# First norm of a decoder step computed on token rows instead of on the transposed input, and expert results read back by two issuing engines

## What is computed

```python
def rms_norm(x, g):
    y = x * lax.rsqrt(jnp.mean(x * x, axis=-1, keepdims=True) + NORM_EPS)
    return y * g

def chunk_spatial_gating(h, w_in, g_v, w_s, b_s, w_out):   # h = rms_norm(x, norm1[0])
    z = jax.nn.gelu(h @ w_in)                # w_in: 1024 x 2048
    u, v = z[..., :CHUNK_WIDTH], z[..., CHUNK_WIDTH:]
    v = rms_norm(v, g_v)
    s = (causal w_s) @ v + b_s               # per chunk of 128 rows and group of 256 columns
    return (u * s) @ w_out, v
# hp = hp + mixer(rms_norm(hp));  hp = hp + experts(rms_norm(hp))
```

## Time and profile before

| | |
|---|---|
| median of 3 runs | 731.02 us (727.8 to 733.04) |
| the profiled execution's own time | 725.12 us |
| its span, first to last instruction | 723.4 us |
| mean granted TensorE clock | 0.952 |
| TensorE products / weight loads busy | 620.2 us (86%) / 422.3 us (58%) |
| VectorE, ScalarE, GpSimd busy | 288.0, 128.8, 126.8 us |

### The profile page before, as it was taken

The page is one execution under the profiler, slowest core; times in us unless marked ns, Lnnn a source line. Parts: engine busy times, 40 slices in busy tenths (PEclk is TensorE's granted clock), DMA queues, the critical chain, the costliest instruction groups (busy, mean ns, idle before and its releaser), DMA issues.

```text
span 723.4 us, 11181 instructions
## 1 busy us (share of the span) xinstructions
PE 620.2 (86%) x4089; PEld 422.3 (58%) x4089; DVE 288.0 (40%) x837; ACT 128.8 (18%) x284; POOL 126.8 (18%) x178
## 2 busy tenths in 40 slices
PE   4899999968999988689999996976987899997730
PEld 2677777746655555566667764564756655564310
DVE  2321232175334422436675775430136434432224
ACT  2102011130111112101121553311114011111100
POOL 0000000002232322004223221320000232331213
PEclk9999999999999999799999999998998999999975
DMA  8985004075899993898333763799736589999633
GB/s 330 291 332 207 27 0 182 6 274 191 339 410 410 410 411 142 305 387 316 117 117 100 257 229 122 252 378 400 310 136 225 192 340 410 412 411 403 232 94 111
DMA packets 60283, 184.81 MB, mean 255 GB/s; under 512 B 11676, under 2 KB 12238, under 8 KB 56006
## 3 DMA queue, kind: packets, MB, share of 16 engines
q1 hardware_dynamic: 49030, 155.52, 57.2%
q0 software_dynamic: 11200, 28.60, 10.9%
HBM read 178.96 MB, written 13.50 MB: 266 GB/s over the span
## 4 chain that ended last, share of the span: by engine, by line
PE 68%; DMA 14%; DVE 9%; SPq 3%; issue 3%; ACT 2%; DVEq 0%; POOLq 0%; ACTq 0%
PE PS L1198 27%; PE PS L1277 11%; DMA hT<-in_moe_w_up 6%; PE PS L1299 6%; PE PS L1446 3%; SPq L367 3%; PE PS L1189 3%; DMA half_b<-in_b_w_o 3%; PE PS L1266 2%; DMA zT<-y_rows 2%; PE PS L1463 2%; DMA y_rows<-zT,where 1%; PE PS L1184 1%; PE PS L1288 1%; PE PS L1256 1%
## 5 line engine op out<-in xcount | busy, mean ns | idle before, releaser
L1198 PE MATMUL PS<-hT,half_b 128*128 128x288 f32 x384 | 101.5, 421 | 8.9 <-DMA half_b<-in_b_w_o 5.6
L1198 PEld LDWEIGHTS PS<-hT,half_b 128*128 128x128 f32 x384 | 74.4, 197 | 32.1 <-issue 10.4
L1198 PE MATMUL PS<-hT,half_a 128*128 128x288 f32 x256 | 66.9, 419 | 3.1 <-DVE hT L799 3.1
L1198 PEld LDWEIGHTS PS<-hT,half_a 128*128 128x128 f32 x256 | 48.7, 194 | 20.9 <-issue 4.1
L539 POOL DMA_INDIRECT y_rows<-zT,where x33 | 33.5, 1015 | 154.0 <-ACT zT L674 148.8
L1277 PE MATMUL PS<-ew_in,zT 128*64 128x256 f32 x480 | 56.0, 387 | 4.8 <-DMA ew_in<-in_moe_w_up 2.9
L942 DVE COPY zT<-PS 128x128 f32<-128x128 f32 x33 | 9.6, 291 | 117.9 <-PE PS L1288 87.7
L1277 PEld LDWEIGHTS PS<-ew_in,zT 128*64 128x64 f32 x480 | 36.7, 140 | 26.3 <-issue 12.6
L534 POOL DMA_INDIRECT zT<-h_rows,where x35 | 36.0, 1030 | 53.6 <-DVE where L911 31.0
L901 DVE TENSOR_SCALAR zT<-lanes,slots 128x128 bf16<-128x128 bf16 (+1 forms) x222 | 39.1, 248 | 1.8 <-DVE slots L964 1.3
L545 POOL DMA_DIRECT2D h_rows<-tokbuf x2 | 1.7, 832 | 216.5 <-ACT tokbuf L657 216.5
(11 more groups left out here) (278 smaller groups left out, 941.9 us busy)
## 6 DMA issues: line engine op xcount, KB each, us to landing
ew_in<-in_moe_w_gate SPq DMA_DIRECT2D x15, 1024.0 KB
ew_in<-in_moe_w_up SPq DMA_DIRECT2D x15, 1024.0 KB
ew_down<-in_moe_w_down SPq DMA_DIRECT2D x15, 1024.0 KB
half_b<-in_moe_w_gate SPq DMA_DIRECT2D x6, 1024.0 KB
half_b<-in_moe_w_up SPq DMA_DIRECT2D x6, 1024.0 KB
half_b<-in_moe_w_down SPq DMA_DIRECT2D x6, 1024.0 KB
half_a<-in_moe_w_gate SPq DMA_DIRECT2D x6, 1024.0 KB
half_a<-in_moe_w_up SPq DMA_DIRECT2D x6, 1024.0 KB
```

Source lines behind the costliest of these rows:

```text
L1198: mm = pe.matmul(PS[:, bank, 0:T], w[:, k, col:col + P], src[:, k, :], start=(k == 0), stop=(k == KT - 1))
```

## The change

The first norm is computed where its sum runs along the row: ScalarE squares the arriving token rows with a running sum, takes three roots' columns, VectorE makes reciprocals per row, and the rows are scaled into `x_scaled` (a view of `zT`), tile 1 by ScalarE, tiles 0 and 2 by VectorE. TensorE transposes the scaled rows, and VectorE applies the gains on the way from PSUM to `hT`. The mean-square products of this norm are gone. The unscaled rows, which the residual needs as `xT`, are transposed in a second set of 8 groups, one behind each V tile of the projection, and ScalarE copies them out between the gelus. Identity is loaded by itself ahead of the gains; the rest of the constants and `ws_in` come behind `w_a`, and the `ws_in` transposes behind the first projection tile. In both layers ScalarE issues the three k = 1 read-backs, SP the three others. The last sums are all VectorE's, and each row tile of the output is written when it is ready.

```diff
@@ SP
-            load(cst[:, :], t["consts"], S["const_in"])
+            load(ident, t["consts"][:, cols["ident"]], S["ident_in"])
...
-            load(ws_in, t["a_w_s"].rearrange("l g t s -> t (l g) s"), S["gains_in"])
             load(w_a, w_in[:, :, D:2 * D], S["w_v_in"])
+            load(cst[:, P:], t["consts"][:, P:], S["const_in"])
+            load(ws_in, t["a_w_s"].rearrange("l g t s -> t (l g) s"), S["const_in"])
             load(w_b, w_in[:, :, 0:D], S["w_u_in"])
...
                 for c, (at, m) in enumerate(tok):
-                    for k, dst in enumerate((tokbuf, y_second)):
-                        load(dst[0:m, c, :], y_dram[l][at:at + m, k, :], s_yb[c])
+                    load(tokbuf[0:m, c, :], y_dram[l][at:at + m, 0, :], s_yb[c])
...
-            sp.wait_ge(S["y_sum"], 1)
-            sp.wait_ge(S["y_sum_pool"], 1)
-            sp.dma_start(o["yp"].rearrange("a (c p) d -> p (a c) d", p=P), tokbuf[:, 0:CH, :]).then_inc(S["y_out"], 16)
-            sp.wait_ge(S["y_sum"], 2)
+            for c in range(CH):
+                sp.wait_ge(S["y_sum"], c + 1)
+                sp.dma_start(o["yp"].rearrange("a (c p) d -> p (a c) d", p=P)[:, c, :], tokbuf[:, c, :]).then_inc(S["y_out"], 16)
+            sp.wait_ge(S["y_sum"], NT)
@@ GpSimd (end)
-            pool.tensor_tensor(tokbuf[:, 1, :], tokbuf[:, 1, :], y_second[:, 1, :], ALU.add).then_inc(S["ysum"], 1)
-            pool.wait_ge(S["ysum"], 1)
-            pool.tensor_tensor(tokbuf[:, 1, :], tokbuf[:, 1, :], x_rows[1], ALU.add).then_inc(S["y_sum_pool"], 1)
@@ ScalarE
+                act.wait_ge(el["sc0"], scattered(LAST - 1)[1])
+                hold(el["sc1"], 16 * more + scattered(LAST - 2)[1])
+                hold(el["in1"], more_gathered(more))
+                hold(el["xt_sb"], more + NE)
+                for c, (at, m) in enumerate(tok):
+                    act.dma_start(y_second[0:m, c, :], y_dram[l][at:at + m, 1, :]).then_inc(s_yb[c], 16)
...
-            squares(0)
-            root(0)
+            ready_for(ACT.Sqrt)
+            act.wait_ge(S["x_in"], 32)
...
+            for c, (_, n) in enumerate(tok):
+                act.activation(squared[c], tokbuf[0:n, c, :], ACT.Square, accum_out=x_sums[0:n, c:c + 1]).then_inc(S["squared"], (3, 3, 2)[c])
+            act.wait_ge(S["squared"], KT)
+            act.activation(x_std[:, 0:CH], x_sums[:, 0:CH], ACT.Sqrt, bias=eps[:, :], scale=1.0 / D)
+            act.activation(x_std[0:TSA, CH:NT], x_sums[0:TSA, CH:NT], ACT.Sqrt, bias=eps[0:TSA, :], scale=1.0 / D).then_inc(S["rooted"], 1)
+            act.wait_ge(S["dve_step"], 1)
+            act.activation(x_scaled[:, 1, :], tokbuf[:, 1, :], ACT.Identity, scale=x_rec[:, 1:2]).then_inc(S["x_row"], 1)
 
             for j in range(2 * KT):
...
+                if j < KT:
+                    act.wait_ge(S["xr_t"], j + 1)
+                    act.copy(xT[:, j, :], PS[:, 4 + j % 2, 0:T]).then_inc(S["xr_sb"], 1)
@@ VectorE
+            dve.wait_ge(S["rooted"], 1)
+            dve.reciprocal(x_rec[:, 0:CH], x_std[:, 0:CH])
+            chain.link(dve.reciprocal(x_rec[0:TSA, CH:NT], x_std[0:TSA, CH:NT]))
+            for c in (0, CH):
+                n = tok[c][1]
+                dve.tensor_scalar(x_scaled[0:n, c, :], tokbuf[0:n, c, :], x_rec[0:n, c:c + 1], None, ALU.mult).then_inc(S["x_row"], 1)
...
-                dve.tensor_copy(xT[:, k, :], PS[:, k % 4, 0:T]).then_inc(S["xt_sb"], 1)
+                dve.tensor_scalar(hT[:, k, :], PS[:, k % 4, 0:T], gains[:, k:k + 1], None, ALU.mult).then_inc(S["normed"], 1)
...
-            norm(0)
...
-            for c, (_, m) in ((0, tok[0]), (CH, tok[CH])):
+            for c, (_, m) in enumerate(tok):
                 dve.wait_ge(s_yb[c], 4 * 16)
@@ TensorE
+            pe.wait_ge(S["x_row"], NT)
             for k in range(KT):
...
-                    mm = pe.transpose(PS[:, k % 4, at:at + n], tokbuf[0:n, c, k * P:(k + 1) * P], ident[0:n, 0:n])
+                    mm = pe.transpose(PS[:, k % 4, at:at + n], x_scaled[0:n, c, k * P:(k + 1) * P], ident[0:n, 0:n])
...
-            mean_squares(0)
...
                 tiles(j % 4, w_a if j < KT else w_b, (j % KT) * P, hT, S["z"],
-                      (lambda k: (S["normed"], k + 1)) if j == 0 else None)
+                      (lambda k: (S["normed"], max(k + 1, 5))) if j == 0 else None)
+                if j == 0:
+                    pe.wait_ge(S["const_in"], 32)
+                    for g in range(4):
+                        mm = pe.transpose(PS[:, 7, g * P:(g + 1) * P], ws_in[:, g, :], ident)
+                    mm.then_inc(S["prep"], 1)
+                if j == 1:
+                    pe.wait_ge(S["prep_sb"], 2)
+                    pe.matmul(PS[0:TSA, 6, 0:4 * TS], spread, wsT[0:TS, :, 0:TS], start=True, stop=True).then_inc(S["prep"], 1)
+                if j < KT:
+                    if j >= 2:
+                        pe.wait_ge(S["xr_sb"], j - 1)
+                    for c, (at, n) in enumerate(tok):
+                        mm = pe.transpose(PS[:, 4 + j % 2, at:at + n], tokbuf[0:n, c, j * P:(j + 1) * P], ident[0:n, 0:n])
+                    mm.then_inc(S["xr_t"], 1)
```

More of the change, by code:

```diff
@@ L203, in hybrid_step @@
         bs_all = shared[:, 0:4 * T].rearrange("p (g n) -> p g n", g=4)
+        x_sums, x_std, x_rec = std[:, 0, 0:NT], std[:, 0, 4:4 + NT], rec[:, 0, 0:NT]
         v_std, v_rec = std[:, 1, 0:NT], rec[:, 1, 0:NT]
@@ L259, in hybrid_step @@
         halves = cst[:, cols["halves"]]
-        names = """x_in w_v_in const_in small_in gains_in pages_in w_u_in w_out_in
-            fill prep prep_sb xt xt_sb squared meansq rooted normed
+        names = """ident_in x_row xr_t xr_sb x_in w_v_in const_in small_in gains_in pages_in w_u_in w_out_in
+            fill prep prep_sb xt squared meansq rooted normed
             z z_sb vtok vtok_sb mixed gated proj res chunk_out
-            logits biased logits_up shifted exped picked counted hrows hrows_sb ysum yt added dve_step
+            logits biased logits_up shifted exped picked counted hrows hrows_sb yt added dve_step
             xrows xrows_sb hrows_t
@@ L324, in source_ready @@
         def source_ready(eng, n, k):
-            if n == 0:
-                eng.wait_ge(S["xt_sb"], k + 1)
-            elif n == 2:
+            if n == 2:
                 eng.wait_ge(S["res"], k + 1)
@@ L518, in _ @@
                 pool.memset(tile[:, :, :], 0.0).then_inc(S["fill"], 1)
-            pool.wait_ge(S["const_in"], 16)
+            pool.wait_ge(S["const_in"], 32)
             pool.tensor_copy(lanes[:, :], cst[:, cols["lanes"]]).then_inc(S["fill"], 1)
@@ L661, in experts, with hold @@
                 el = E[l]
+                def hold(s, value):
+                    act.wait_ge(s, value)
+                    act.sem_inc(S["held"], 1)
                 def gate(q):
@@ L1014, in _ @@
             chain.link(dve.reciprocal(v_rec[0:TSA, CH:NT], v_std[0:TSA, CH:NT]))
+            dve.wait_ge(S["xr_t"], KT)
             for i in range(2 * NT):
@@ L1025, in _ @@
                 dve.tensor_tensor(uT[:, j, :], sq[:, j, :], uT[:, j, :], ALU.mult).then_inc(S["gated"], 1)
+            dve.wait_ge(S["xr_sb"], KT)
             project(0)
@@ L1334, in experts @@
                     rows_up(q + 1, 16 * i + gathered(LAST + 2)[1], q + 1)
-            pe.wait_ge(S["const_in"], 16)
-            pe.wait_ge(S["x_in"], 32)
+            pe.wait_ge(S["ident_in"], 16)
+            pe.wait_ge(S["gains_in"], 16 * 5)
+            pe.transpose(PS[:, 6, 0:5 * KT + 2], gain_rows[:, :], ident[0:5 * KT + 2, 0:5 * KT + 2]).then_inc(S["prep"], 1)
+            pe.wait_ge(S["x_row"], NT)
             for k in range(KT):
                 if k >= 4:
-                    pe.wait_ge(S["xt_sb"], k - 3)
+                    pe.wait_ge(S["normed"], k - 3)
                 for c, (at, n) in enumerate(tok):
-                    mm = pe.transpose(PS[:, k % 4, at:at + n], tokbuf[0:n, c, k * P:(k + 1) * P], ident[0:n, 0:n])
+                    mm = pe.transpose(PS[:, k % 4, at:at + n], x_scaled[0:n, c, k * P:(k + 1) * P], ident[0:n, 0:n])
                 mm.then_inc(S["xt"], 1)
-                if k == 0:
-                    pe.wait_ge(S["gains_in"], 16 * 6)
-                    pe.transpose(PS[:, 6, 0:5 * KT + 2], gain_rows[:, :], ident[0:5 * KT + 2, 0:5 * KT + 2]).then_inc(S["prep"], 1)
-            for j in range(4):
-                mm = pe.transpose(PS[:, 5, j * P:(j + 1) * P], ws_in[:, j, :], ident)
-            mm.then_inc(S["prep"], 1)
-            pe.wait_ge(S["fill"], 5)
-            mean_squares(0)
-            pe.wait_ge(S["prep_sb"], 2)
-            pe.matmul(PS[0:TSA, 6, 0:4 * TS], spread, wsT[0:TS, :, 0:TS], start=True, stop=True).then_inc(S["prep"], 1)
             def value_squares():
@@ L1383, in _ @@
                     pe.wait_ge(S["w_u_in"], 16)
-                pe.wait_ge(S["z_sb"], j - 3) if j >= 4 else pe.wait_ge(S["xt_sb"], KT)
+                if j >= 4:
+                    pe.wait_ge(S["z_sb"], j - 3)
```

(7 more changed lines are left out.)

16 lines of the change are left out of this document (8 added, 8 removed).

## The result

| | before | after |
|---|---|---|
| median (runs) | 729.41 us (4) | 719.26 us (4) |
| profiled execution | 725.12 us | 718.64 us |
| its span | 723.4 us | 716.9 us |

The ratio is 0.9856, with a 95% interval of 0.9819 to 0.9893: faster by 1.4%, 10.2 us. In the two profiles the last read-back is first issued at 699.24 us before and at 700.99 after, so up to there the changed kernel is 1.75 us behind, and all of its shorter span comes after that point.

The account below looks back on a forecast made before the run. It took the chain of waits as the bound, all three changed places lying on it: +1.2 (start) - 0.9 (layer 0 read-back) - 3.9 (tail) = -3.6 us, profiled 725.1 to 721.5; median forecast 727.4, range 719.5 to 733.

Parts of the forecast that it names:

- the tail: Last stage: sums and earlier landing save 2.8 us, output 1.1; together -3.9 us (bounds -2.1 and -4.8).
- The start: Up to U tile 8: saves 5.5 us ahead of the projection, puts 6.7 into it; a loss of 1.2 us.
- the interleaved groups: Eight transpose groups between the projection's V tiles: 0.7 us each, 5.6 in all (bounds 4.2 and 8.6).
- a bias product: In the projection, tiles 4 to 7: 0.88 us each, four of them.
- The `spread` product: Behind tile 1 of the projection: costs 0.9 us, priced like a bias product.
- tile 0: First projection tile: still pays a cold clock, 1.5 us above the warm 3.88 (bounds 0.5 and 3).
- `ws_in`: Its four transposes, moved behind the first projection tile: 0.5 us at the upper clock.
- The cheap groups: Rival: groups at 0.53 us, start gains about 1.7, both read-backs at 400 GB/s; sum -8.3, 722.7; chance 0.17.
- I let a shift at the start run through undiminished: From the start to the end: a shift at the start counts in full, though expert weights and attention pages limit the middle.
- The read-back of layer 0: Layer 0's end: two issuers shorten the 2.36 MB read by 0.9 us (bounds 0 and 1.8).
- The third rival: Two queues bring nothing: both read-backs land as before; sum -1.7 us, 729.3; chance 0.22.
- the second, weights in the way: Rival, layer 0: `w_qkv` loads slow ScalarE's transfers, landing 5.5 us later; sum +2.8, 733.8; chance 0.08.

Follow-up runs that it names:

- sums_moved: The kernel before with only the three last sums moved to VectorE, the two-tile output still one 1 MB transfer; ratio 0.9910.
- front_only: The kernel before with only the start changed: first norm on token rows, its transposes and the order of loads; ratio 0.9992.
- squares_spread: The changed kernel with the 48 one-column products that square-sum V spread behind tiles instead of one block; 716.85 us, ratio 0.9831.
- tail_only: The kernel before with only the last stage changed: all last sums on VectorE, each output row tile written when ready; ratio 0.9906.
- read_only: The kernel before with only the second expert's rows read back on ScalarE's queue, in both layers; ratio 0.9974.
- before_spread: The kernel before with only the 48 one-column square-sum products of V spread behind tiles; ratio 0.9987.
- both: The changed kernel with the square-sum products spread and layer 1's sample tile read back, summed and written first; 716.09 us, ratio 0.9796 to the kernel before.

## Why the prediction was wrong

**The step that failed** is the tail, in its sentence "GpSimd's removed work was on this path only". By my own rows `ys` landed at 715.37 + 3.5 = 718.9 and the span ended at 723.4, and I did not ask what filled the 4.5 us; I ended the chain with `ys`. What ended last was GpSimd's drain, 8.9 us behind its last sum, so that sum lay on a second path, to the end of the span. Taking it away cut SP's last wait from 4.3 us to 0.2. The tail gained 8.3 us where I had -3.9 with bounds of -2.1 and -4.8.

The rest of the tail came out as worked: from tile 1's landing to the last sum's end 6.7 us before (715.35 - 708.66) and 4.85 after (714.58 - 709.73), 1.8 saved, as forecast; tile 1 landed 0.7 sooner after the first issue (8.74 and 9.42), where I had 0.9 to 1.1; `ys` landed in 1.9 instead of 3.5, 1.6 saved for my 1.1. Together 4.1, and with 4.1 of drain 8.2. But the reason I gave for `ys` held only in part: `sums_moved`, with `yp` in one piece, has 2.2. VectorE's sums beside GpSimd's take 2.63 and 3.25 in the earlier trace rows and 1.2 in every kernel that has moved them.

**The start** had the wrong sign. U tile 8 began 2.6 us earlier, at 59.38, where I had 63.3. Of the 3.9 between:

- rows landed at 6.8, 0.4 sooner, and the three squares took 3.2, not 3.8: their accumulator read lies beside the next square, so that one takes 1.06. The first transpose started at 12.3 instead of 13.4. The scaling took 0.70 each for 0.75. The transposes took 6.95 for 6.9, so the projection was 1.0 ahead at 19.3.
- the interleaved groups cost 0.59 each (4.47 from the tile at 30.36 to the next at 34.83, less 3.88) and not 0.7. In the chain that is 0.39 for the group and 0.20 by which the tile behind it is longer; for eight groups and seven such tiles, 4.5 instead of 5.6: 1.1.
- a bias product, beside a group, cost 0.57 (V tiles are 5.04 apart, less 4.47) and not the 0.88 of the earlier trace rows, which holds the 0.20 of the tile behind: 1.2 for four. The `spread` product, priced like it, cost 0.3: 0.6 less.
- tile 0 (5.48 for 5.38) and `ws_in` (0.44 for 0.5) were right.

That is 1.0 + 1.1 + 1.2 + 0.6 = 3.9. The errors all lie on one side, and several terms lie outside the bounds that I had given: the squares at 3.2 (3.8 to 4.35), the first transpose at 12.3 (12.9 to 14.8), the projection at 19.3 (19.6 to 21.7), and the whole start at -2.6 (-1.7 to +5). The groups (4.5 in 4.2 to 8.6) and tile 0's extra (1.6 in 0.5 to 3) lie inside. That TensorE would not wait for ScalarE's copies was right: it has no gap in this stretch.

None of the rivals was right as a whole. The cheap groups' price of 722.7 came nearest. For the start alone it was the better picture (groups at 0.53 against 0.59 measured and my 0.7, a start 1.7 us shorter against 2.6), but `front_only` shows no measurable gain from the start, and the rival has no drain. That its total lies near is luck.

And the sentence "I let a shift at the start run through undiminished" was wrong: of 2.6 us at tile 8, 1.1 was left at the output projection, and nothing measurable at the end, where `front_only` is level with before. The 1.5 us are given back to the clock's lower level in and behind the one-column products; `squares_spread` shows the clock at 1.00 without the block. What takes the rest further on is not settled. In single profiles the layer 0 read-back is issued at 289.9 to 294.1 in the five kernels with the old start and at 290.75 to 293.8 in the nine with the new, so 1 us could not be told there anyway. The changed kernel's expert tiles at 268 and 284 us take longer than the ones before, at a granted clock of 0.68 and 0.54 where the kernel before has 1.00:

```profile
268.01 5.25 PE PS L1300 x32
...
284.61 3.46 PE PS L1322 x8
```

(3.67 and 1.95 us in the chain of before.) That isn't the change's doing: the first takes 5.2 to 5.4 us in six of the fourteen profiles, `tail_only` and `read_only` with the old start among them, and 3.67 in the others; the second takes 1.95 in the kernel before and `before_spread` only, and 2.6 to 3.5 in the twelve others.

**The read-back of layer 0** was forecast right: first issue to landing is 8.3 us, before 9.0 (299.58 - 290.61); `read_only` has 8.5. That is 0.7 for my 0.9. Over all profiles it is 9.0 to 9.9 us in the five kernels that issue on one queue and 8.15 to 8.65 in the nine that issue on two. In the chain:

```profile
292.94 7.89 DMA zT<-y_rows
```

The third rival, two queues that bring nothing, falls with these landings, which don't overlap, and with `read_only`, thinly (its interval ends at 0.9995); the second, weights in the way, falls too: the landing did not slip. The rule of the Trainium skill ("DMA: Bandwidth & Descriptors", Issuing engines are not separate DMA queues), that issuing from several engines saves only the time to initiate, fits the small size of the gain. I had read it as a term of 0, but the time to initiate is itself something: here six issues take 3.1 us on one queue (699.24 to 702.36) and 1.3 on two. Between 2 and 7 us behind the first issue the engines moved 296 to 326 GB/s from one queue (four kernels) and 401 to 410 from two (three kernels with the same order of tiles), which doesn't say whether the issues or something else held them back. The Trainium skill's other rule ("TensorE: Matmul & The Clock Gate", Part 4), that transposes do not bring the upper clock, held by the pace: tile 0 took 5.5 to 6.9 us in the nine kernels with the new start, 3.88 being its time at the upper level. The view's clock doesn't show it: it stands at 1.00 from 20 to 22 us of the changed kernel, though TensorE makes 4 instructions in each of these microseconds, as at 0.50 from 27 to 29 in the kernel before, and 6 at 1.00. In the earlier trace rows too it is 1.00 over the mean squares that I called slow, so the lower level in the first 20 us rests on the pace alone.

## What to carry to other kernels

Follow the chain to the span's last microsecond, and where the last transfer lands before it, look at the closing instructions of every engine: here an engine that did its last bit of work late held the program 4 us, and taking that work from it was worth more than the time of the work. If an engine has a long drain, give it its last instruction early. And a gain on a path through TensorE is only worth what is left behind the next place where the clock falls. Look for blocks of narrow products behind the place you speed up; spreading them kept the clock up in three traces, though no measured time here shows that it pays at the end.

## What the runs showed of the hardware

GpSimd's closing drain takes 8.9 to 9.0 us, after a 0.09 us memset as after a DMA issue, and 12.1 when it is reached while a sum of 3.2 is still running, which is again 8.9 behind that sum. The other engines' drains end within 0.1 us of their last instruction: VectorE's takes 1.25 beside a last sum of 1.21 (3.28 beside one of 3.25), TensorE's 2.2 (3.8 in `both`, whose last products are slower), ScalarE's 0.15 when it is idle. The wait for a drain may be shown under another engine's name.

Two-input sums of 1024 columns on VectorE and GpSimd, at the same time, take 2.3 to 3.3 us where VectorE alone takes 1.2: the last four sums took 6.7 us on the two engines (from 708.66) and 4.85 on VectorE alone.

A block of 48 instructions with one column, 4.06 to 4.79 us in which TensorE is never idle (4.00 of 4.00 busy), brings the lower clock in all eleven profiles that have it: the granted clock falls 2.9 to 4.7 us behind the block's start and is back at 1.00 after 3.4 or 6.8 us. In the three kernels where they are spread between tiles of 288 columns it stays at 1.00.
